# Two feed-forward layers in split fp32: block copies one tile later, weight rests first in odd tiles, statistics begun before the last products

## The chip, the cores and the metric

The kernel is one program on one core of a Trainium2 chip. The engines are TensorE (PE in the profile, PEld its weight loads), VectorE (DVE), ScalarE (ACT), GpSimd (POOL) and SyncE (SP, which issues most of the transfers). The metric is the device time of one execution in microseconds; less is better. Of the runs shown here the median counts.

## The reference, cut to what matters

A model of three layers on 512 tokens of width 1024, all in float32. Layer 0 has stick-breaking attention, layer 1 sparse attention on shared keys and values, and the last layer, which adds 16 meta tokens, has differential and grouped attention and a mixture of 16 experts. The change touches the two dense feed-forward layers, which end layers 0 and 1, and what follows each of them:

```python
def sqrelu_mlp(x, w1, w2):
    h = jax.nn.relu(x @ w1)
    return (h * h) @ w2
...
    h = h + sqrelu_mlp(rms_norm(h, norm_gain[layer, 1]), mlp_w1[layer], mlp_w2[layer])
...
return rms_norm(h, final_norm)
```

`w1` is 1024 x 4096 and `w2` 4096 x 1024. After layer 0 comes the norm of the shared keys and values. After layer 1 come two norms in a row: the first model's final norm, and then the norm `g_mix_2` that begins the last layer, whose input also holds 16 rows of meta tokens.

## The kernel before, in words

**Split numbers.** A float32 matrix product is made of three products of numbers rounded to fp32r. Each operand x is held as an upper part (a rounded copy) and a rest (x less the upper part). `mm3` (L2863) issues upper by upper, upper by rest, rest by upper. So for every operand ScalarE writes the upper part first, and VectorE then subtracts it to get the rest; TensorE needs both.

**A feed-forward layer** (m = 0 or 1) is cut in four parts (f = 0 to 3) of 1024 hidden columns. A part has two halves:
- *hidden tiles* j = 0 to 7 (`hidden` in `ff_pe`): 24 matmuls each. ScalarE makes the relu (L3099), VectorE multiplies for the square `hid_sq` (L3258).
- *products* q = 0 to 6 (`product` in `ff_pe`): the second matrix product is done by a Strassen-like scheme on 2 x 2 blocks, with seven products of 24 matmuls each. It needs sums and differences of hidden blocks (`sums`, L3242 to L3253, four short VectorE operations for each pair of tiles) and of weight blocks (`turn`, L3267, VectorE, two for each c = 0 to 3).

For a pair i of hidden tiles (2i and 2i + 1) four *block copies* n = 0 to 3 are needed. ScalarE's is `piece_upper` (L3082 to L3089), VectorE's is `piece_lower` (L3236 to L3240). Copy 0 is from the square of the even tile, copy 1 from that of the odd tile, copies 2 and 3 are those of the block sums, made after `sums`. Product 0 needs copy 0, product 1 needs copy 3, later products need the others.

**Weights.** Part f uses 22 weight buffers in a row, n = 0 to 21: one for each hidden tile, then two for each product (product q takes n = 8 + 2q and 9 + 2q). Each is loaded by SyncE to a ring of eight slots (or made by `turn`), gets its upper part from ScalarE (`ff_upper`, L2964) and its rest from VectorE (`ff_lower`, L2982), in one of four split buffers. So buffer n can be written when TensorE is through with n - 4: weight 8 in hidden tile 4, weight 12 after product 0. `ff_upper_freed` waits for that. TensorE waits for the rest with `split_w`.

**Order on VectorE** (`ff_dve`). Every engine has one fixed order of instructions. In hidden tile j: square, copy 0 or 1 of the pair, rest of weight j + 4, and in odd tiles the sums and copies 2 and 3. `turn(f, 0, n)` comes after tiles 4 and 6, `turn(f, 1, n)` for both n after tile 7. Then for each product q: `taken` (L3284) adds the two finished output banks to `h`, and then come the rests of weights 12 + 2q and 13 + 2q (of the next part where n passes 21). ScalarE's order mirrors it (`ff_act`). GpSimd only counts ring slots free (`ff_pool`), the last time when the rest of weight 21 is made.

**The end of a layer.** In layer 0 all seven products of the last part are taken in `ff_dve`, and then norm 2 follows (`flow_act`, `flow_pool`, `norm_dve`): squares of the two 512-wide halves of each 128-token tile on ScalarE, three short GpSimd operations for the reciprocal root, the scaled copy `xn` on ScalarE, eight transposes on TensorE. In layer 1 the last two products (`leave` = 2) are taken by `residual` in `flow2_dve`, mixed with the scaling of the first norm (`plain`, L660); `flow2_act` loads its table of functions, squares the meta tokens' tile, squares the first halves of all four tiles, scales the meta tile, and then works tile by tile through both norms. The `g_mix_2` norm goes in the order meta tile, 0, 1, 2, 3, and each tile's columns are split in two pieces (`x_hi` L778 on ScalarE, `x_lo` L785 on VectorE), ten pieces in all. TensorE begins the first projection of the differential attention (`df_parts`, L1568) when all splits are there; it does 24 matmuls for columns 0 to 263 and then 24 for columns 264 to 527. SyncE loads constants for the last layer after TensorE's last feed-forward matmul, and then further weights.

## Time and profile before

| | |
|---|---|
| median of 3 runs | 2543.26 us (2541.18 to 2544.34) |
| profiled execution | 2541.81 us, of which the span from first to last instruction is 2539.8 us |
| mean granted TensorE clock | 0.978 of full speed |
| busy: PE, DVE, ACT, POOL | 2377.6, 1606.2, 1100.4, 754.0 us |
| feed-forward layer 0 | from 318 to 656 us of the span |
| feed-forward layer 1 | from about 1060 to 1398 us |
| DMA | 268.46 MB, mean 106 GB/s |

Times below are microseconds from the start of the span. In a row of the timeline stand start, duration, engine, line, operation, what is written and what is read, shape and count; in brackets is how long the engine sat idle before it, and what released it. Successive matmuls overlap: each is shown at its full duration, and the next one starts before it ends.

### The profile page before, as it was taken

The numbers are of one execution on the slowest core, as the hardware profiler recorded it, in microseconds if no ns is written. First come the engines' busy times: TensorE is split into PE (matmuls) and PEld (weight loads), VectorE is DVE, ScalarE is ACT, GpSimd is POOL, SyncE is SP. The second block draws the span as 40 slices with busy tenths as digits, with TensorE's granted clock in tenths as the row PEclk, the third lists the DMA queues.
The fourth block names the chain that finished last, engine by engine and source line by source line (L and its number), as shares of the span: only waits on it lengthen the run. The fifth ranks groups of instructions, "written<-read, shape, count | busy, mean of one in ns | idle before, by whom it ended". The sixth has DMA issues, their size and how long they took to land.

```text
span 2539.8 us, 36841 instructions
## 1 busy us (share of the span) xinstructions
PE 2377.6 (94%) x13845; PEld 1890.6 (74%) x13845; DVE 1606.2 (63%) x2449; ACT 1100.4 (43%) x1986; POOL 754.0 (30%) x851
## 2 busy tenths in 40 slices
PE   7999899999999898999999799989999899899998
PEld 6777788777577665777877688879989797555555
DVE  3333277787564786487777666762067643588888
ACT  4444344444321575344445333341145401267776
POOL 7654400000007003400000644435742276411112
PEclk9999999999999899999999899999999999899999
DMA  4111223332323000332331211112210022389998
GB/s 136 53 56 50 80 79 117 116 89 78 104 88 99 18 1 7 111 83 83 116 116 43 71 51 43 46 55 67 83 42 26 26 92 87 134 290 366 362 364 300
DMA packets 267748, 268.46 MB, mean 106 GB/s; under 512 B 13258, under 2 KB 198437, under 8 KB 267603
## 3 DMA queue, kind: packets, MB, share of 16 engines
q1 hardware_dynamic: 263075, 254.04, 31.2%
q0 software_dynamic: 4528, 12.44, 1.9%
q8 instruction: 96, 1.57, 0.3%
q14 instruction: 49, 0.40, 0.1%
HBM read 256.24 MB, written 10.21 MB: 105 GB/s over the span
## 4 chain that ended last, share of the span: by engine, by line
PE 67%; DVE 16%; ACT 6%; DMA 5%; issue 5%; POOL 2%; SPq 0%; DVEq 0%; POOLq 0%; ACTq 0%
PE psum L2865 12%; PE psum L2868 12%; PE psum L2869 12%; DMA ex_tile<-in_w_down 5%; PE psum L1539 2%; PE psum L2503 2%; PE psum L2569 2%; ACT w_hi L2964 2%; PE psum L872 2%; PE psum L1254 2%; PE psum L874 2%; DVE w_lo L2982 2%; PE psum L873 2%; PE psum L1317 1%; PE psum L1309 1%
## 5 line engine op out<-in xcount | busy, mean ns | idle before, releaser
L2865 PE MATMUL psum<-x_hi,w_hi 128*128 128x264 f32 (+2 forms) x1560 | 527.2, 338 | 20.9 <-DVE x_lo L785 7.2
L2868 PE MATMUL psum<-x_lo,w_hi 128*128 128x264 f32 (+2 forms) x1560 | 517.9, 332 | 0.0
L824 POOL TENSOR_TENSOR w_hi<-ring_tile,one 128x256 fp32r<-128x256 f32 (+1 forms) x284 | 235.9, 858 | 461.0 <-PE psum L2869 429.5
L2869 PE MATMUL psum<-x_hi,ring_tile_lo 128*128 128x264 f32 (+2 forms) x1096 | 340.7, 311 | 0.0
L2865 PEld LDWEIGHTS psum<-x_hi,w_hi 128*128 128x128 f32 x1560 | 296.1, 190 | 55.9 <-issue 21.1
L2868 PEld LDWEIGHTS psum<-x_lo,w_hi 128*128 128x128 f32 x1560 | 296.3, 190 | 27.6 <-issue 1.2
L828 POOL TENSOR_TENSOR ring_tile_lo<-ring_tile,w_hi 128x256 fp32r<-128x256 f32 (+1 forms) x284 | 294.8, 1065 | 8.1
L2869 PEld LDWEIGHTS psum<-x_hi,ring_tile_lo 128*128 128x128 f32 x1096 | 208.1, 190 | 11.2
L2869 PE MATMUL psum<-x_hi,w_lo 128*128 128x512 f32 (+1 forms) x528 | 202.4, 383 | 0.0
L2865 PE MATMUL psum<-w_hi,hid_hi 128*128 128x512 f32 x448 | 176.4, 394 | 13.0 <-DVE w_lo L2982 13.0
L2964 ACT ACTIVATE w_hi<-ring_tile 128x1024 fp32r<-128x1024 f32 x128 | 130.8, 1050 | 123.2 <-PE psum L2869 112.5
L2868 PE MATMUL psum<-w_lo,hid_hi 128*128 128x512 f32 x448 | 176.7, 394 | 0.0
L2869 PE MATMUL psum<-w_hi,hid_lo 128*128 128x512 f32 x448 | 175.7, 392 | 0.0
L2982 DVE TENSOR_TENSOR w_lo<-ring_tile,w_hi 128x1024 fp32r<-128x1024 f32 x124 | 148.3, 1221 | 26.9 <-ACT w_hi L2964 26.9
L2353 DVE TENSOR_TENSOR ex_tile_lo<-ex_tile,ex_w_hi 128x1024 fp32r<-128x1024 f32 x128 | 149.5, 1218 | 15.1 <-ACT ex_w_hi L2346 13.6
L2346 ACT ACTIVATE ex_w_hi<-ex_tile 128x1024 fp32r<-128x1024 f32 x128 | 129.7, 1056 | 26.7 <-DMA ex_tile<-in_w_gate 12.4
L3088 ACT ACTIVATE hid_hi<-hid_sq 128x512 fp32r<-128x512 f32 (+1 forms) x128 | 70.5, 575 | 140.4 <-DVE hid_sq L3251 81.4
L2328 PE MATMUL psum<-ex_tile_lo,xs_hi 128*66 128x512 f32 x256 | 103.2, 403 | 15.1 <-DVE ex_tile_lo L2353 9.3
L2869 PEld LDWEIGHTS psum<-x_hi,w_lo 128*128 128x128 f32 x528 | 99.6, 189 | 19.4
L2865 PEld LDWEIGHTS psum<-w_hi,hid_hi 128*128 128x128 f32 x448 | 84.1, 188 | 35.9 <-issue 16.3
L734 POOL TENSOR_TENSOR rstd<-ssq 128x1 f32<-128x1 f32 x12 | 2.3, 191 | 357.7 <-ACT junk_ff L693 351.8
L3239 DVE TENSOR_TENSOR hid_lo<-hid_sq,hid_hi 128x512 fp32r<-128x512 f32 (+1 forms) x128 | 77.2, 624 | 45.5 <-ACT hid_hi L3088 45.5
(454 smaller groups left out, 5529.5 us busy)
## 6 DMA issues: line engine op xcount, KB each, us to landing
ring_tile<-in_mlp_w SPq DMA_DIRECT2D x128, 512.0 KB, 4.1
ex_tile<-in_w_gate SPq DMA_DIRECT2D x64, 512.0 KB, 12.4
ex_tile<-in_w_up SPq DMA_DIRECT2D x64, 512.0 KB, 12.0
ex_tile<-in_w_down SPq DMA_DIRECT2D x64, 512.0 KB, 12.0
ring_tile<-in_w_in SPq DMA_DIRECT2D x52, 512.0 KB, 3.8
ring_tile<-in_sb_w_qkv SPq DMA_DIRECT2D x24, 512.0 KB, 3.8
ring_tile<-in_nsa_w_kv SPq DMA_DIRECT2D x12, 512.0 KB, 3.8
ring_tile<-in_sb_w_o SPq DMA_DIRECT2D x8, 512.0 KB, 3.3
```

What stands on the lines that cost most here:

```text
L824: last = pool.tensor_tensor(hi[:, cols], raw[:, cols], one[:, :].broadcast_to([P, D // len(parts)]), ALU.mult)
L828: last = pool.tensor_tensor(lo[:, cols], raw[:, cols], hi[:, cols].bitcast(F32), ALU.subtract)
L2328: first = pe.matmul(dst, xs_hi[:, u, k, :], lo[:, k % 2, :], start=(k == 0), stop=False)
L2346: act.activation(ex_w_hi[:, n, :], ex_ring.wait(act, name, j + n, turn), ACT.Copy).then_inc(ex_wh, 1)
L2353: dve.tensor_tensor(ex_tile_lo[:, slot, :], ex_tile[:, slot, :], ex_w_hi[:, n, :].bitcast(F32), ALU.subtract).then_inc(ex_ws, 1)
L2865: upper = pe.matmul(dst, a_hi, b_hi, start=first, stop=False, skip_group_check=True)
L2868: pe.matmul(dst, a_hi, b_lo, start=False, stop=False, skip_group_check=True)
L2869: return pe.matmul(dst, a_lo, b_hi, start=False, stop=final, skip_group_check=True)
L2964: act.activation(hi, raw, ACT.Copy).then_inc(split_w_hi, 1)
L2982: eng.tensor_tensor(lo, raw, hi.bitcast(F32), ALU.subtract).then_inc(split_w, 1)
L3088: act.activation(hid_piece(hid_hi[i], first, last), sq_piece(i, half, rows).rearrange("p (a n) -> p a n", n=SEQ // 2), ACT.Copy).then_inc( ...
L3239: dve.tensor_tensor(hid_piece(hid_lo[i], first, last), sq_piece(i, half, rows).rearrange("p (a n) -> p a n", n=SEQ // 2), hid_piece(hid_hi ...
```

## The change

In the hidden tiles of both layers, copies 2 and 3 of a pair, upper parts and rests alike, move from the odd tile that makes the sums to the even tile after it (for the last pair, to behind the eight tiles). In odd tiles the upper part and the rest of weight j + 4 come ahead of copy 1. `turn(f, 0, 1)` moves from tile 6 to tile 4, `turn(f, 1, 0)` from behind tile 7 to tile 6; `turn(f, 1, 1)` stays behind the tiles.

In the last part, `taken` of product 5 is cut in two: its first half (tile 0) comes between the rests of weights 20 and 21, for both layers. In layer 0 the rest follows as before; in layer 1 it is left to `flow2_dve`, which no longer has `residual(0)`.

ScalarE gets a piece of the next norm ahead of the upper parts of weights 20 and 21 of the last part: the table load and the first half-squares of tiles 0 and 1, and in layer 1 also the meta tile's square.

TensorE's first projection of the differential attention waits only for 8 of the 10 splits (meta tile and tiles 0 to 2) before its first 24 matmuls, and for all 10 before the next 24.

```diff
--- before.py
+++ after.py
@@ -597,7 +597,7 @@
         def place(u, t):
             return PLACE[t] if u == 6 else t
 
-        def flow2_act(act):
+        def flow2_act(act, first=False):
 
             def square(u, t, c):
                 r = rows_of(t)
@@ -620,12 +620,18 @@
                     act.wait_ge(norm_tp, 2 * (norm_base(6) + n - 1))
                 act.activation(xn[0:r, n % 2, :], h[0:r, t, :], ACT.Copy, scale=rstd[0:r, t:t + 1]).then_inc(norm_xn, 1)
 
-            act.preload_act_table_set(LN_EXP)
-            whole(6, QT)
-            act.wait_ge(norm_sq, squared(6, QT))
-            for t in range(QT):
-                act_t.inc(square(5, t, 0))
-                act.wait_ge(act_step, act_t.value())
+            def halves(tiles):
+                for t in tiles:
+                    act_t.inc(square(5, t, 0))
+                    act.wait_ge(act_step, act_t.value())
+
+            if first:
+                act.preload_act_table_set(LN_EXP)
+                whole(6, QT)
+                act.wait_ge(norm_sq, squared(6, QT))
+                halves(range(2))
+                return
+            halves(range(2, QT))
             scaled(QT)
             for s in range(8):
                 if s < QT:
@@ -663,7 +669,6 @@
                 residual_tile(dve, H_ALL - UPD, 1, t, half_banks)
 
             dve.wait_ge(gain_in, 16)
-            residual(0)
             residual(1)
             plain(0)
             residual(2)
@@ -679,12 +684,8 @@
 
         HALVED = (1, 2, 4, 5, 7)
 
-        def flow_act(act, u, updated=None):
-
-            base, halves = norm_base(u), u in HALVED
-            act.preload_act_table_set(LN_EXP)
-
-            def square(t, c):
+        def flow_square(act, u, updated, t, c):
+                halves = u in HALVED
                 cols = slice(c * D // 2, (c + 1) * D // 2) if halves else slice(0, D)
                 if u == 0:
                     act.wait_ge(tile_in[t], 16)
@@ -693,10 +694,22 @@
                 return act.activation((junk if u in (0, 1) else junk_ff)[:, cols], h[:, t, cols], ACT.Square, scale=D ** -0.5,
                                       accum_out=ssq[:, c, t:t + 1])
 
+        def first_squares(act, u, updated, tiles):
+            for t in tiles:
+                act_t.inc(flow_square(act, u, updated, t, 0))
+                act.wait_ge(act_step, act_t.value())
+
+        def flow_act(act, u, updated=None, begun=0):
+
+            base, halves = norm_base(u), u in HALVED
+            if not begun:
+                act.preload_act_table_set(LN_EXP)
+
+            def square(t, c):
+                return flow_square(act, u, updated, t, c)
+
             if halves:
-                for t in range(QT):
-                    act_t.inc(square(t, 0))
-                    act.wait_ge(act_step, act_t.value())
+                first_squares(act, u, updated, range(begun, QT))
             if u in FF_NORMS:
                 for j in range(2):
                     if u == 1:
@@ -1570,6 +1583,8 @@
             for n in range(3):
                 w = split2_wait(pe, "df", 4 * hd + n, 0, SPLIT_BASE["df"] + hd * 3 + n, w2_hi[:, (hd + n) % 2, :])
                 for c in range(2):
+                    if hd == n == 0 and c:
+                        pe.wait_ge(split_x, split_base(7))
                     if n == 0 and c == 0:
                         pe.wait_ge(v2_l, hd + 1)
                     elif hd == 0:
@@ -3028,7 +3043,7 @@
             pe.wait_ge(norm_ev, 2 * (norm_base(6) + T2))
             pe.wait_ge(ff_freed, 2)
             ring.wait(pe, "df", 6)
-            pe.wait_ge(split_x, split_base(7))
+            pe.wait_ge(split_x, split_base(6) + 2 * QT)
             for _ in df_parts(pe, 0):
                 pass
             pe.wait_ge(b2_ready, 1)
@@ -3078,7 +3093,7 @@
         HID_PIECES = (("A11", "A11", 0, slice(0, SEQ // 2)), ("A12", "A22", 1, slice(0, SEQ)),
                       ("S2", "S3", 0, slice(0, SEQ)), ("S4", "S1", 1, slice(0, SEQ)))
 
-        def ff_act(act, m, upd):
+        def ff_act(act, m, upd, early):
             def piece_upper(f, i, n):
                 first, last, half, rows = HID_PIECES[n]
                 if n < 2:
@@ -3097,12 +3112,19 @@
                     act.wait_ge(ff_mm, n + 1)
                     act.wait_ge(ff_hid, n + 3)
                     act.activation(relu[:, j % 2, :], ff_hid_bank(f, j)[:, :], ACT.Relu).then_inc(ff_relu, 1)
+                    if j % 2 == 0 and j:
+                        piece_upper(f, j // 2 - 1, 2)
+                        piece_upper(f, j // 2 - 1, 3)
+                    if j % 2:
+                        ff_upper_freed(act, m, upd, f, j + SPLITS)
                     piece_upper(f, j // 2, j % 2)
-                    ff_upper_freed(act, m, upd, f, j + SPLITS)
-                    if j % 2:
-                        piece_upper(f, j // 2, 2)
-                        piece_upper(f, j // 2, 3)
+                    if j % 2 == 0:
+                        ff_upper_freed(act, m, upd, f, j + SPLITS)
+                piece_upper(f, FF_PAIRS - 1, 2)
+                piece_upper(f, FF_PAIRS - 1, 3)
                 for q in range(len(PRODUCTS)):
+                    if f == FF_PARTS - 1 and q == 4:
+                        early()
                     for n in (FF_TILES + SPLITS + 2 * q, FF_TILES + SPLITS + 2 * q + 1):
                         if n < FF_STREAM:
                             ff_upper_freed(act, m, upd, f, n)
@@ -3122,15 +3144,19 @@
             for p in range(PAIRS):
                 sb_act(act, p)
             flow_act(act, 1, H_BEFORE[1] - QT)
-            ff_act(act, 0, UPD)
-            flow_act(act, 2, H_BEFORE[2] - QT)
+            def second_norm():
+                act.preload_act_table_set(LN_EXP)
+                first_squares(act, 2, H_BEFORE[2] - QT, range(2))
+
+            ff_act(act, 0, UPD, second_norm)
+            flow_act(act, 2, H_BEFORE[2] - QT, 2)
             kv_act(act)
             gates_act(act)
             act.preload_act_table_set(LN_EXP)
             queries_act(act)
             nsa_act(act)
             flow_act(act, 4, H_BEFORE[4] - QT)
-            ff_act(act, 1, H_BEFORE[4])
+            ff_act(act, 1, H_BEFORE[4], lambda: flow2_act(act, True))
             flow2_act(act)
             act.wait_ge(b2_in, B2_CONST)
             act.wait_ge(lam_d, 1)
@@ -3257,12 +3283,15 @@
                 dve.wait_ge(ff_relu, n + 5)
                 dve.scalar_tensor_tensor(hid_sq[:, i % 2, j % 2, :], ff_hid_bank(f, j)[:, :], 0.0, relu[:, j % 2, :],
                                          ALU.max, ALU.mult).then_inc(ff_hid, 1)
-                piece_lower(f, i, j % 2)
+                if j % 2 == 0 and j:
+                    piece_lower(f, i - 1, 2)
+                    piece_lower(f, i - 1, 3)
+                if j % 2 == 0:
+                    piece_lower(f, i, 0)
                 lower(f, j + SPLITS)
                 if j % 2:
+                    piece_lower(f, i, 1)
                     sums(f, i)
-                    piece_lower(f, i, 2)
-                    piece_lower(f, i, 3)
 
             def turn(f, c, n):
                 first = ff_raw(dve, m, f, (B12, B22, B22, B21)[c] + n)
@@ -3270,7 +3299,7 @@
                 dst = ff_difference(m, f, n) if c == 2 else w2_turn[:, n, :]
                 dve.tensor_tensor(dst, first, other, ALU.subtract).then_inc(ff_t, 1)
 
-            def taken(f, q):
+            def taken(f, q, which=(0, 1)):
                 n, rows = ((1, (0, 1)), (0, (2, 3)), (0, (0, 1)), (0, (0, 1)), (0, (2, 3)), (1, (0, 1)), (1, (2, 3)))[q]
                 name = PRODUCTS[q][1]
                 if q < 3:
@@ -3278,6 +3307,8 @@
                 elif q == 3:
                     dve.wait_ge(ff_ev, EV_0 + ff_part(m, f, 3) + 3)
                 for c, t in enumerate(rows):
+                    if c not in which:
+                        continue
                     if q >= 3:
                         dve.wait_ge(acc_done, upd + f * UPD + n * QT + t + 1)
                     hs = h[:, t, 512 * n:512 * n + 512]
@@ -3292,17 +3323,27 @@
             for f in range(FF_PARTS):
                 for j in range(FF_TILES):
                     hidden(f, j)
-                    if j in (4, 6):
-                        turn(f, 0, (j - 4) // 2)
-                for n in range(2):
-                    turn(f, 1, n)
-                for q in range(len(PRODUCTS) - (leave if f == FF_PARTS - 1 else 0)):
+                    if j == 4:
+                        turn(f, 0, 0)
+                        turn(f, 0, 1)
+                    if j == 6:
+                        turn(f, 1, 0)
+                last = f == FF_PARTS - 1
+                piece_lower(f, FF_PAIRS - 1, 2)
+                piece_lower(f, FF_PAIRS - 1, 3)
+                turn(f, 1, 1)
+                for q in range(len(PRODUCTS) - (2 if last else 0)):
                     taken(f, q)
                     for n in range(2):
+                        if last and q == 4 and n:
+                            taken(f, 5, (0,))
                         lower(f, FF_TILES + SPLITS + 2 * q + n)
                     if q in (1, 3):
                         for n in range(2):
                             turn(f, 2 if q == 1 else 3, n)
+            if not leave:
+                taken(FF_PARTS - 1, 5, (1,))
+                taken(FF_PARTS - 1, 6)
 
         @block.vector
         def _(dve):
```

## Rows read from the trace of the kernel before

**Rows 1.** Waits of PE, whole span: total, times, longest in us.
```profile
PE psum L2865 <- DVE w_lo L2982: 13.0, 8, 1.6
...
PE psum L2865 <- DVE x_lo L785: 7.2, 3, 6.6
```

**Rows 2.** Busy time by stretch, from one such wait's end to the next.
```profile
375.49:459.71 84.22, 82.59 (x360) 67.52 (x361) 65.07 (x85) 35.00 (x47) 0.00 (x0) 1.00 0.34 100
```

**Rows 3.** Timeline of PE around product 2 of the first part.
```profile
373.46 0.40 PE L2869 MATMUL psum<-w_hi,hid_lo 128*128 128x512 f32 x1
375.49 0.48 PE L2865 MATMUL psum<-w_hi,hid_hi 128*128 128x512 f32 x1 [1.63 <-DVE w_lo L2982]
375.80 0.40 PE L2868 MATMUL psum<-w_lo,hid_hi 128*128 128x512 f32 x1
```

**Rows 4.** Timeline of DVE, first part, tile 7 to product 2.
```profile
363.94 0.68 DVE L3258 SCALAR_TENSOR_TENSOR hid_sq<-psum,relu 128x512 f32<-128x512 f32 x1
...
367.41 0.42 DVE L3247 TENSOR_TENSOR hid_sq<-hid_sq 128x256 f32<-128x256 f32 x1
...
369.45 1.29 DVE L3239 TENSOR_TENSOR hid_lo<-hid_sq,hid_hi 128x512 fp32r<-128x512 f32 x2 [0.24 <-ACT hid_hi L3088]
370.66 2.35 DVE L3271 TENSOR_TENSOR w_turn<-ring_tile,w_turn 128x1024 f32<-128x1024 f32 x2
372.93 1.28 DVE L3284 TENSOR_TENSOR h<-psum,h 128x512 f32<-128x512 f32 x2
374.13 2.35 DVE L2982 TENSOR_TENSOR w_lo<-w_turn,w_hi 128x1024 fp32r<-128x1024 f32 x2
```

**Rows 5.** Timeline of ACT, the relu of tile 7 in the first part.
```profile
362.83 0.60 ACT L3099 ACTIVATE relu<-psum 128x512 f32<-128x512 f32 x1 [1.20 <-PE psum L2869]
```

**Rows 6.** Timeline of ACT, POOL and DVE at the end of layer 1's feed-forward.
```profile
1381.18 2.01 ACT L2964 ACTIVATE w_hi<-ring_tile 128x1024 fp32r<-128x1024 f32 x2 [3.51 <-PE psum L2869]
...
1386.73 2.01 ACT L2964 ACTIVATE w_hi<-w_turn 128x1024 fp32r<-128x1024 f32 x2 [3.53 <-PE psum L2869]
...
1388.02 2.35 DVE L2982 TENSOR_TENSOR w_lo<-w_turn,w_hi 128x1024 fp32r<-128x1024 f32 x2
...
1388.75 1.28 ACT L623 ACT_TABLE_LOAD   x1
...
1391.23 0.63 ACT L609 ACTIVATE junk_ff<-h 128x512 f32<-128x512 f32 x1
1391.28 0.22 POOL L651 TENSOR_SCALAR rstd<-ssq 128x1 f32<-128x1 f32 x1 [335.01 <-ACT junk_ff L609]
...
1391.59 0.57 POOL L653 TENSOR_TENSOR rstd<-rstd,neg_half 128x1 f32<-128x1 f32 x1
...
1392.29 0.69 DVE L3221 TENSOR_TENSOR h<-psum,h 128x512 f32<-128x512 f32 x1 [1.32 <-PE psum L2869]
...
1394.25 1.15 ACT L621 ACTIVATE xn<-h,rstd 16x1024 f32<-16x1024 f32 x1
...
1395.31 0.61 ACT L609 ACTIVATE junk_ff<-h 128x512 f32<-128x512 f32 x1
```

**Rows 7.** Timeline of all engines, first transposes of tile 0 after layer 1.
```profile
1402.94 1.97 PE L796 MATMUL psum<-ident,xn 128*128 128x128 f32 x8 [4.52 <-ACT xn L621]
```

**Rows 8.** The chain that ended last, up to the first projection.
```profile
1417.58 2.12 DVE x_lo L785 x2
```

**Rows 9.** Timeline of PE, the first projection's first matmuls.
```profile
1420.06 0.56 PE L2865 MATMUL psum<-x_hi,w_hi 128*128 128x264 f32 x1 [6.61 <-DVE x_lo L785]
...
1423.44 0.28 PE L2865 MATMUL psum<-x_hi,w_hi 128*128 128x264 f32 x1
1423.56 0.28 PE L2868 MATMUL psum<-x_lo,w_hi 128*128 128x264 f32 x1
```

**Rows 10.** Busy time by stretch ahead of it: engines, then PEclk, DMA share, GB/s.
```profile
1415.00:1418.00 3.00, 0.00 (x0) 0.00 (x0) 3.00 (x5) 1.23 (x2) 3.00 (x4) 0.76 0.00 0
```

**Rows 11.** Timeline of DVE at the end of layer 0's feed-forward.
```profile
656.21 0.69 DVE L3284 TENSOR_TENSOR h<-psum,h 128x512 f32<-128x512 f32 x1 [2.10 <-PE psum L2869]
```

## The prediction

> **What bounds the kernel now.** I read the page's busy shares first: TensorE is at work for 94% of the span, so only what shortens TensorE's idle time, or the work around it, can move the end. Then the waits of TensorE over the whole span [rows 1]. The reader is to see one reason that returns: eight waits for a weight's rest (L2982), 13.0 us together, none over 1.63. A view of TensorE's gaps puts one in each feed-forward part, always ahead of product 2. The stretches from one to the next are 84.22 us long with 82.59 of work [rows 2]; that is one of six, 84.21 to 84.24. The other wait of size is a single one of 6.61 us for `x_lo`, ahead of the attention of the last layer [rows 9]; before it stands one of 4.52 us for the scaled tile 0 [rows 7].
>
> **Why product 2 waits.** In the first part ScalarE's relu of tile 7 ends at 363.43 [rows 5]. VectorE starts the square only at 363.94, because `turn` was in its way, and then works without a real pause: sums from 367.41, copies 2 and 3 from 369.45, two turns from 370.66, take of product 0 from 372.93, rest of weight 12 from 374.13 [rows 4]. TensorE's last matmul of product 1 starts at 373.46 and the next at 375.49 [rows 3].
>
> **What one such stall is worth.** The profile's 1.63 us counts from the end of a matmul that the next one would have overlapped. Matmuls start 0.23 us apart, though each shows 0.40: 84.22 less the stall is some 82.4 for 360 of them, 0.229 [rows 2]. Without the wait the next would start at 373.69, so 1.80 is lost; the first behind it holds up its successor by 0.31 in place of 0.23 [rows 3], another 0.08. I take 1.88 for each part. From below it is the 1.63 of the idle column.
>
> **Part 1: the new order in hidden tiles.** Nothing is added: each part has the same copies, sums, turns and rests. What goes is VectorE's waiting for ScalarE between its own steps. Start-to-start times from [rows 4]: a turn or a rest 1.14 (370.66 to 372.93 is two), the take of two banks 1.20, two copies 1.21 (369.45 to 370.66), a square 0.61 (half of that pair, same size), four sums with the wait to copy 2 2.04 (367.41 to 369.45). New sequence behind tile 7, with one `turn` gone from tile 6: square at 363.46 (relu's end and 0.03). ScalarE copies weight 11 at once, 363.34 to 364.38, 1.04 as in [rows 6] (2.01 for two, which overlap a little); rest 11 at 364.42; copy 1 at 365.56, its end 0.69 later at 366.25; sums at 366.28 and so copies 2 and 3 at 368.32; `turn(f, 1, 1)` at 369.53; take of product 0 at 370.66; rest 12 at 371.86, done at 373.08. The release of TensorE took 0.14 in the old order (374.13 + 1.22 to 375.49), so weight 12 is there at 373.22, and 373.69 is when TensorE can want it. The stall goes, with 0.47 us in hand. Is VectorE behind before tile 7? In tile 4 it now has square 0.61, copies 2 and 3 1.21, copy 0 0.4, rest 1.14 with some 0.3 of waiting, two turns 2.27: 5.9 for a tile of 24 x 0.229 = 5.5; tile 5 has square, rest, copy 1 and sums, 0.61 + 1.14 + 0.65 + 1.8 (the 2.04 less its 0.24 of waiting) = 4.2, and makes up the 0.4. Tile 6 has one turn, 4.8. So tile 7 starts on time. Ring loads are no obstacle: weight 12's slot is freed by the rest of weight 4, six tiles ahead of the turn that now reads it.
>
> **What is late next.** Product 1 needs copy 3 of the last pair for its last quarter, a quarter of 24 matmuls before 373.69, at 372.3; its rest ends at 369.61. Behind product 2 every VectorE step is 2.3 us earlier than before and TensorE 1.9, so no later product gets tighter; they had no wait. Gain of this part 8 x 1.88 = 15.0 us; bounds 13.0 (idle column), and if the 0.47 in hand were not there but 0.5 lacking, 8 x 1.4 = 11.
>
> **Part 2: cover in the last part.** Product 5's first half ends one half product before its second, which VectorE sees at 1392.29: 12 x 0.23 earlier is 1389.51. The early statistics run on ScalarE from 1383.20 (behind the pair of 1381.18) and take, from the old places, table and meta square 2.48 (1388.75 to 1391.23) and two half-squares of 0.755 (four were 3.02, 1391.23 to 1394.25): until 1387.20, against 1386.73 for the old start of weights 20 and 21 [rows 6]. Rest 20 then starts at 1388.28 (0.26 late), the take of tile 0 at 1389.51, rest 21 at 1390.11, ready at 1391.47. Product 6 can start at 1392.09. So the layer's last product doesn't wait, with 0.6 in hand; in layer 0 there is no meta square, and more in hand.
>
> The Trainium skill ("ScalarE: Activation LUTs", What ACT_TABLE_LOAD costs) gives a table load some 1.38 us of draining behind its 1.28, for a switch of sets. Here the next instruction follows at 1.30, meta square and all inside the 2.48. By the page the early work would end 1.38 later and product 6 wait some 0.6 us at the end of layer 1; by the rows it doesn't.
>
> **Part 3: what the early work earns.** In layer 0 the transposes of tiles 0 and 1 wait for nothing but TensorE's own last product; the chain then goes from that product through VectorE's take at 656.21 [rows 11], the gains, ScalarE's raw copies, and only then the third tile's square. None of it starts earlier. Gain 0. In layer 1 TensorE's products end at 1397.8 (1392.29 and 24 x 0.23), but the chain lies on ScalarE: weights 20 and 21, table, meta square, four half-squares, meta scaling at 1394.25, tile 0's second half at 1395.31 [rows 6]. New: weights done at 1389.2, two half-squares until 1390.7. Then the meta scaling needs GpSimd's root, and GpSimd is held in its counting loop until rest 21 is done, 1391.33; its two operations took 0.88 (1391.28 to 1392.16), so 1392.25 at best; scaling 1.06; tile 0's half-square at 1393.4. That is 1.9 earlier; I take 1.8 for GpSimd's release. Everything behind goes in the same order and shifts along (TensorE's final banks are there at 1395.1 and 1397.9, before they are taken). Bounds: 0, were a hidden wait next, and 3.5, were GpSimd not in the way.
>
> **Part 4: the projection.** TensorE now waits for eight splits, not ten. The last two take 2.12 us [rows 8], so it starts at 1417.94, or 1416.14 with part 3, in place of 1420.06. Columns 0 to 263 lie in tiles 0 to 2, and the next 24 matmuls come over 2.9 us later, when the last splits (1418.0 by then) are done. The DMAs, tied to the last product and so not shifted, are over before 1415 [rows 10]. Gain 2.1, from 1.9 (half of four pieces) to 2.12. The granted clock was at its lower level, 1.2 GHz, for the first 15 matmuls, 0.225 apart, then 2.4 with 0.12 [rows 9], after the idle stretch before it [rows 10]. That costs 15 x 0.105 = 1.6 now; with a shorter idle stretch (4.6 in place of 6.6) it can be from 0 to 2.5 (all 24). I take the same.
>
> The Trainium skill ("TensorE: Matmul & The Clock Gate", HAM oscillation) lets an idle stretch drop the clock; if the shorter one no longer did, 1.6 more would be won.
>
> **Sum.** 15.0 + 1.8 + 2.1 = 18.9 us off the profiled execution's 2541.81 (its span and 2.0 around it), 2522.9. The median of the runs lies 1.45 above that execution; from 2543.26 the same sum gives 2524.4. After this the kernel's later stages follow TensorE and each other, so they move as a whole.
>
> **The rivals.**
> - *The stalls stay in part.* 0.47 us in hand is one short VectorE operation. For it: all eight parts have it alike, so 0.1 missing costs 0.8. Against it: the durations hardly vary. With 0.5 to 1.5 left per part, 2528 to 2536; 2530 as its centre. Chance 0.13.
> - *The ends earn nothing.* Rest 21 or GpSimd's root comes later than reckoned, product 6 waits, and the chain to `x_lo` doesn't move: parts 3 and 4 give 0 to 2, time 2526.5 to 2528.5. The page's drain is of this kind, 2525. For it: GpSimd's 335 us of waiting ends at [rows 6] only by the meta square, so its release by rest 21 was never seen. Chance 0.08.
> - *The clock pays.* No drop in part 4, and other drops fall elsewhere: 2520 to 2523. The spread of three runs before is 3.2. Chance 0.07.
> - *Slower: copy 3 of the last pair comes too late for product 1.* The place is behind tile 7, where copies 2 and 3 now stand in both queues. I have 2.7 us in hand. Were the copies 6.6 late (a tile, 5.5, and a turn), product 1 would stall 3.9 in each part, 31 us: 2555.6. It outweighs the 18.9 from a stall of 2.4 on, so from 5.1 us of lateness. Against it: everything ahead of these copies is ready earlier than now. Chance 0.02.
> - *The change doesn't do what it says*: product 2's stall is as long, because another step of VectorE's fills the time. Only the ends move: 2539. Chance 0.03.
>
> **How the numbers follow.** My forecast, all of parts 1 to 4, has 0.67; time 2524.4, own range 2522.5 to 2527. The range goes down to the clock's rival and up into the partial stalls: 2520.5 to 2532. About what a measurement can tell from no change is 0.2%, 5 us: 2538.2 to 2548.3. Inside it lie most of "doesn't do what it says" and a tail of the first rival, 0.04; above it 0.02; below 0.94.
>
> **What the new profile would show.** No wait for L2982 in TensorE's list; stretches from one product 2 to the next of 82.3 us; `hid_sq` of tile 7 0.03 behind its relu; VectorE idle 2 us more in products. At layer 1's end: the table load before weights 20 and 21, tile 0's second half-square some 1.9 us nearer to the last product, the wait ahead of the first transposes 2.7 in place of 4.52, the wait ahead of the projection 4.5 in place of 6.6. Wrong would be: a new wait of L2865 for `hid_lo`, a wait of product 6 for rest 21, or an unchanged end with the stalls gone, which would mean a later stage has its own clock.

## The result and the profile after

The changed kernel takes 2524.28 us, the median of 5 runs (2522.70 to 2525.09). The kernel before, run beside it, takes 2542.01 us (5 runs, 2535.99 to 2544.34). The ratio is 0.9932, with a 95% interval of 0.9917 to 0.9946: faster, by 17.7 us. The profiled execution of the changed kernel took 2525.02 us with a span of 2523.2, against 2541.81 and 2539.8 before.

TensorE's waits over the whole span, the lines that answer to [rows 1, 7, 9]:

```profile
PE psum L809 <- ACT xn L621: 6.1, 3, 2.9
...
PE psum L2880 <- DVE x_lo L798: 5.1, 3, 4.5
```

The eight waits for a weight's rest, 13.0 us of idle time, are gone from the list, and the single wait ahead of the last layer's projection has shrunk from 6.6 to 4.5. The stretch from the first part's product 2 to the second's, which answers to [rows 2], is now all work, and 1.87 shorter:

```profile
373.26:455.61 82.35, 82.35 (x362) 67.62 (x360) 64.89 (x85) 34.27 (x46) 0.00 (x0) 1.00 0.35 103
```

All six such stretches measure 82.35. VectorE's timeline behind tile 7, which answers to [rows 4]:

```profile
363.02 0.69 DVE L3284 SCALAR_TENSOR_TENSOR hid_sq<-psum,relu 128x512 f32<-128x512 f32 x1 [0.79 <-ACT relu L3114]
...
363.97 1.23 DVE L2997 TENSOR_TENSOR w_lo<-w_turn,w_hi 128x1024 fp32r<-128x1024 f32 x1 [0.26 <-ACT w_hi L2979]
...
367.88 1.29 DVE L3265 TENSOR_TENSOR hid_lo<-hid_sq,hid_hi 128x512 fp32r<-128x512 f32 x2 [0.24 <-ACT hid_hi L3103]
369.09 1.22 DVE L3300 TENSOR_TENSOR w_turn<-ring_tile,w_turn 128x1024 f32<-128x1024 f32 x1
370.23 1.28 DVE L3315 TENSOR_TENSOR h<-psum,h 128x512 f32<-128x512 f32 x2
371.43 2.35 DVE L2997 TENSOR_TENSOR w_lo<-w_turn,w_hi 128x1024 fp32r<-128x1024 f32 x2
```

The square now follows its relu, and has idled 0.79 for it: VectorE is in time. Rest 12 starts 8.41 behind the square, where it was 10.19 before. It is done 1.22 into the last row, at 372.65, which with the release of 0.14 makes weight 12 ready at 372.79. TensorE takes it up when its own order allows:

```profile
373.03 0.39 PE L2884 MATMUL psum<-w_hi,hid_lo 128*128 128x512 f32 x1
373.26 0.39 PE L2880 MATMUL psum<-w_hi,hid_hi 128*128 128x512 f32 x1
```

These answer to [rows 3]: 0.23 from one start to the next, no idle time, and 0.47 us between 372.79 and 373.26.

At the end of layer 1, the timeline of ScalarE, VectorE and GpSimd that answers to [rows 6]:

```profile
1368.87 1.28 ACT L629 ACT_TABLE_LOAD   x1
1370.17 1.06 ACT L609 ACTIVATE junk_ff<-h 16x1024 f32<-16x1024 f32 x1
...
1372.86 2.01 ACT L2979 ACTIVATE w_hi<-w_turn 128x1024 fp32r<-128x1024 f32 x2
...
1375.18 0.69 DVE L3315 TENSOR_TENSOR h<-psum,h 128x512 f32<-128x512 f32 x1
1375.79 1.22 DVE L2997 TENSOR_TENSOR w_lo<-w_turn,w_hi 128x1024 fp32r<-128x1024 f32 x1
...
1377.28 0.22 POOL L657 TENSOR_SCALAR rstd<-ssq 128x1 f32<-128x1 f32 x1 [327.27 <-DVE w_lo L2997]
...
1378.24 1.15 ACT L621 ACTIVATE xn<-h,rstd 16x1024 f32<-16x1024 f32 x1 [2.01 <-POOL rstd L659]
1379.30 0.61 ACT L609 ACTIVATE junk_ff<-h 128x512 f32<-128x512 f32 x1
```

The table load stands ahead of weights 20 and 21, which start at 1372.86. GpSimd, held before by the meta square [rows 6], is now released by VectorE's rest 21, and ScalarE idles 2.01 us for GpSimd's root before it scales the meta tile. TensorE's rows behind it, which answer to [rows 7, 9]:

```profile
1386.94 1.09 PE L809 MATMUL psum<-ident,xn 128*128 128x128 f32 x8 [2.85 <-ACT xn L621]
...
1402.01 0.56 PE L2880 MATMUL psum<-x_hi,w_hi 128*128 128x264 f32 x1 [4.49 <-DVE x_lo L798]
...
1404.79 0.42 PE L2880 MATMUL psum<-x_hi,w_hi 128*128 128x264 f32 x1
...
1405.33 0.28 PE L2880 MATMUL psum<-x_hi,w_hi 128*128 128x264 f32 x1
```

The idle times are 2.85 for 4.52, and 4.49 for 6.61. The projection still begins at the lower clock (1.2 GHz): matmuls start some 0.22 apart until 1405.01, then 0.12, 14 of them slow where there were 15. The granted clock was 0.50 of full speed from 1402 to 1405.

### The profile page after: what moved, and what is told of

Same layout as the page of the kernel before. It is cut to its first block, busy times and chain, and to the rows that moved or that the text cites. A ratio compares the mean times of both kernels' runs of the same rounds, so it can differ in the third digit from the quotient of the medians.

```text
span 2523.2 us, 36839 instructions
## 1 busy us (share of the span) xinstructions
PE 2374.5 (94%) x13845; PEld 1890.0 (75%) x13845; DVE 1605.6 (64%) x2449; ACT 1093.6 (43%) x1986; POOL 745.8 (30%) x851
## 4 chain that ended last, share of the span: by engine, by line
PE 77%; DVE 10%; DMA 6%; ACT 3%; issue 3%; POOL 2%; SPq 0%; DVEq 0%; POOLq 0%; ACTq 0%
PE psum L2880 16%; PE psum L2883 16%; PE psum L2884 16%; DMA ex_tile<-in_w_down 5%; PE psum L1552 2%; PE psum L2518 2%; PE psum L2584 2%; PE psum L885 2%; PE psum L1267 2%; PE psum L887 2%; PE psum L886 2%; PE psum L1330 1%; PE psum L1322 1%; PE psum L2527 1%; PE psum L2343 1%
## 5 line engine op out<-in xcount | busy, mean ns | idle before, releaser
L2880 PE MATMUL psum<-x_hi,w_hi 128*128 128x264 f32 (+2 forms) x1560 | 527.2, 338 | 18.9 <-DVE k_lo L1816 7.1
L3114 ACT ACTIVATE relu<-psum 128x512 f32<-128x512 f32 x64 | 38.3, 598 | 189.8 <-PE psum L2884 189.8
L2348 PE MATMUL psum<-ex_w_hi,xs_lo 128*66 128x512 f32 x256 | 101.8, 398 | 0.0
L2349 PE MATMUL psum<-ex_w_hi,xs_hi 128*66 128x512 f32 x256 | 101.5, 396 | 0.0
```

Of the source, the lines that this page charges most:

```text
L2348: pe.matmul(dst, xs_lo[:, u, k, :], hi[:, k % 2, :], start=False, stop=False)
L2349: last = pe.matmul(dst, xs_hi[:, u, k, :], hi[:, k % 2, :], start=False, stop=(k == KT - 1))
L2880: upper = pe.matmul(dst, a_hi, b_hi, start=first, stop=False, skip_group_check=True)
```

## The experiments

Three lengths are read from TensorE's timeline in each kernel: a *part* (product 2 to the next part's product 2, all six), the *end* (first matmul of the last product 2 to tile 0's first transposes, layer 1), and the *projection* (from those transposes to the first matmul of the projection). The end starts just behind the last stall. So in a kernel with stalls it also holds the 0.08 by which a stall delays the second matmul [rows 3]. That is why 33.16 stands beside 33.07, and 31.45 to 31.49 beside 31.38, with nothing else different.

| kernel | part | end | projection | median, lowest to highest | ratio to before (95%) |
|---|---|---|---|---|---|
| before | 84.22 | 33.16 | 17.11 | 2542.01, above | |
| changed | 82.35 | 31.38 | 15.08 | 2524.28, above | 0.9932 (0.9917 to 0.9946) |
| order only | 82.35 | 33.07 | 17.13 | 2526.34, 2522.39 to 2527.87 | 0.9948 (0.9931 to 0.9966) |
| ends only | 84.23 | 31.45 | 15.08 | 2535.08, 2530.92 to 2538.65 | 0.9985 (0.9975 to 0.9995) |
| turns back | 83.08 | 31.48 | 15.10 | 2529.47, 2528.86 to 2530.61 | 0.9962 (0.9950 to 0.9975) |
| turns only | 84.23 | 33.16 | 17.10 | 2539.89, one run | |
| nothing early in layer 0 | 82.35 | 31.38 | 15.07 | 2522.63, 2522.08 to 2523.91 | 0.9939 (0.9922 to 0.9955) |
| odd tiles back | 82.62 | 31.49 | 15.09 | 2523.84, 2522.05 to 2525.88 | 0.9922 (0.9905 to 0.9938) |
| short operation added | 82.35 | 31.37 | 15.07 | 2521.55, one run | |
| long operation added | 83.09 | 31.48 | 15.09 | 2530.01, 2529.60 to 2531.31 | 0.9948 (0.9931 to 0.9964) |
| root early | 82.35 | 29.70 | 15.29 | 2521.61, 2519.68 to 2524.06 | 0.9913 (0.9896 to 0.9929) |
| root early, no load wait | 82.35 | 29.70 | 14.94 | 2522.88, 2521.52 to 2524.30 | 0.9920 (0.9906 to 0.9933) |
| changed again | 82.35 | 31.40 | 15.10 | 2522.08, 2518.04 to 2523.09 | 0.9910 (0.9895 to 0.9925) |

The kernel before, run in three groups, gave 2539.27 (2535.24 to 2543.97) beside order only, ends only, turns back and nothing early in layer 0; 2543.19 (2537.7 to 2544.6) beside odd tiles back, the two added operations and root early; and 2542.68 (2535.95 to 2546.65) beside the other three. The lengths above hold within 0.04 in every part; the medians of the kernel before move by 4 us.

### The order alone

The kernel before with the new order of copies, rests and turns in the hidden tiles, and nothing at the layers' ends.

```diff
 # kernel before: hidden() and ff_act() with the changed order
+                if j % 2 == 0 and j:
+                    piece_lower(f, i - 1, 2)
+                    piece_lower(f, i - 1, 3)
...
+                    if j == 4:
+                        turn(f, 0, 0)
+                        turn(f, 0, 1)
+                    if j == 6:
+                        turn(f, 1, 0)
```

> The kernel before with the new order in the hidden tiles alone (copies, weight rests, turns); layer ends and the projection's wait as before. My account: the wait of TensorE for the rest of weight 12 is gone in all eight parts, 1.88 us each, so 15.0 us less than before (about 2528 where before is 2543); the stretch from one product 2 to the next is 82.3 us; the wait ahead of the first transposes of tile 0 after layer 1 stays 4.5 and that ahead of the projection 6.6. Rival (the parts aren't independent, the order needs the shorter ends): less than 13 us. Rival (part of the gain comes from elsewhere): more than 16 us.

The parts are 82.35 long as in the changed kernel, the end and the projection as in the kernel before. TensorE's waits in this kernel:

```profile
PE psum L2865 <- DVE x_lo L785: 7.5, 3, 6.9
...
PE psum L796 <- ACT xn L621: 6.9, 3, 4.5
```

The two waits of the ends stay, 6.9 and 4.5, and no wait for a weight's rest is left. The order alone takes away all the stalls of the parts.

The median fell by 12.9 and not by 15.0, which by the number alone is the rival's case (less than 13). The trace speaks against the rival's reason, since the stalls are gone without the shorter ends. Where the other 2 us may be is told in the last section: in stretches behind the feed-forward layers that were longer here.

### The ends alone

The changed kernel with the old order in the hidden tiles: early squares, the cover in the last part, and eight splits ahead of the projection remain.

```diff
 # changed kernel: hidden() and ff_act() back to the old order
-                if j % 2 == 0 and j:
-                    piece_lower(f, i - 1, 2)
-                    piece_lower(f, i - 1, 3)
...
+                    if j in (4, 6):
+                        turn(f, 0, (j - 4) // 2)
```

> The changed kernel with the old order in the hidden tiles: early statistics, product 5 taken in two halves, and the projection's shorter wait stay. My account: eight waits for the rest of weight 12, 1.6 us each in the idle column, stretches of 84.2 us; from the layer end 1.8 us and from the projection 2.0, 3.8 us less than before in all, which is below what a timing can tell (0.2%) but plain in the trace. Rival (the ends earn nothing by themselves): the two waits stay 4.5 and 6.6 us.

```profile
PE psum L2880 <- DVE w_lo L2997: 13.1, 8, 1.6
```

That line of TensorE's waits is [rows 1] again, while end and projection are 1.7 and 2.0 shorter. Each set of edits keeps its own saving without the other: 1.87 in each part for the order, 3.7 at the end of layer 1 for the ends (1.71 and 2.03). By the medians they are worth 12.9 and 4.2 against the kernel before run beside them, 17.1 together where both at once gave 17.7.

### The turns at their old places

```diff
 # changed kernel
-                    if j == 4:
-                        turn(f, 0, 0)
-                        turn(f, 0, 1)
-                    if j == 6:
-                        turn(f, 1, 0)
+                    if j in (4, 6):
+                        turn(f, 0, (j - 4) // 2)
...
-                turn(f, 1, 1)
+                for n in range(2):
+                    turn(f, 1, n)
```

> The changed kernel, with the turns at their old places: turn(f, 0, 1) after tile 6 and both turn(f, 1, n) behind the last copies. My account by the same sum: two turns behind the copies put the rest of weight 12 at 374.36 on the first part's old scale, where TensorE wants it at 373.69, so a stall of 0.67 and 0.08 behind it returns in each part: 6.0 us more than the changed kernel. Rival (the copies' move alone removed the stall, the turns are off the path): no difference, under 1 us. Rival (the turns' move alone did it): the full 15 us come back.

```profile
373.79:456.89 83.10, 82.61 (x360) 67.52 (x361) 64.98 (x85) 34.29 (x47) 0.00 (x0) 1.00 0.34 102
```

This is the stretch by engine of the first part. A second turn behind tile 7 costs 1.14 on VectorE, 0.47 was in hand, and this part is 0.75 longer (0.71 to 0.75 over the six). TensorE's idle column grows by 0.49 only (83.10 less 82.61).

### The turns alone

The kernel before with the turns at their new places and the old order of copies and rests.

```diff
 # kernel before
-                    if j in (4, 6):
-                        turn(f, 0, (j - 4) // 2)
-                for n in range(2):
-                    turn(f, 1, n)
+                    if j == 4:
+                        turn(f, 0, 0)
+                        turn(f, 0, 1)
+                    if j == 6:
+                        turn(f, 1, 0)
+                turn(f, 1, 1)
```

> The kernel before with only the turns at their new places (both turn(f, 0, n) after tile 4, turn(f, 1, 0) after tile 6), copies and weight order as before. My account: VectorE has no slack in tiles 4 to 7 in the old order, 4.4 us of steps and waits for an even tile with one turn and 6.7 for an odd one, 11.1 for 11.0 of TensorE's, so a turn moved ahead only pushes the rest back: the step from one product 2 to the next stays 84.2 us, and the square of tile 7 comes 1.1 later. Rival (moving the turn away from product 2 is what helps): 83.1 us a part.

The stall before product 2 stands unchanged, at the end of tile 7's chain:

```profile
374.72 0.47 PE L2865 MATMUL psum<-w_hi,hid_hi 128*128 128x512 f32 x1 [1.63 <-DVE w_lo L2982]
```

```profile
362.06 0.60 ACT L3099 ACTIVATE relu<-psum 128x512 f32<-128x512 f32 x1
```

```profile
363.17 1.22 DVE L3271 TENSOR_TENSOR w_turn<-ring_tile,w_turn 128x1024 f32<-128x1024 f32 x1
364.31 0.68 DVE L3258 SCALAR_TENSOR_TENSOR hid_sq<-psum,relu 128x512 f32<-128x512 f32 x1
```

On VectorE the turn now placed in tile 6 starts at 363.17, because tile 6 runs late. The relu of tile 7 ends at 362.66, and the square starts at 364.31, 1.65 behind it, where it was 0.51 in the kernel before (363.94 behind 363.43 [rows 4, 5]). One turn fewer behind tile 7 is paid for by one turn that still stands in tile 7's way. By itself the move of the turns is worth nothing; with the new order of copies and rests it is worth 0.75 a part.

### The odd tiles as before

The changed kernel, but in odd tiles the block's first copy again ahead of the weight's rest, on both engines.

```diff
 # changed kernel, ff_act (hidden() in the same way)
-                    if j % 2:
-                        ff_upper_freed(act, m, upd, f, j + SPLITS)
                     piece_upper(f, j // 2, j % 2)
-                    if j % 2 == 0:
-                        ff_upper_freed(act, m, upd, f, j + SPLITS)
+                    ff_upper_freed(act, m, upd, f, j + SPLITS)
```

> The changed kernel, except that in odd tiles copy 1 comes before the upper part and the rest of weight j + 4 again, as it was; the copies one tile later and the turns' new places stay. My account: VectorE waits again for ScalarE inside tile 7, 0.66 us in all, so the rest of weight 12 is ready at 373.88 on the first part's old scale against the 373.69 that TensorE can use: each part some 0.2 to 0.27 us longer than in the changed kernel, 2 us in all, though the idle column shows next to nothing. Rival (the order in odd tiles carries a third of the gain or more): 5 us or more. Rival (it is idle decoration): 0.

```profile
373.47:456.10 82.63, 82.61 (x360) 67.53 (x361) 64.81 (x85) 34.63 (x46) 0.00 (x0) 1.00 0.34 102
```

The part is 0.27 longer, with 0.02 of idle time shown. So this edit is worth 0.27 of the 1.88 a part, 2.2 us over the eight, too little to be told in the medians here.

### How much is in hand: a short and a long operation

A VectorE addition into a buffer that nothing reads any more, ahead of the turn behind tile 7. It adds work to the computation and changes no output.

```diff
 # changed kernel; the long one with relu[:, :, :]
+                dve.tensor_tensor(relu[:, 1, 0:256], relu[:, 1, 0:256], relu[:, 1, 0:256], ALU.add)
                 turn(f, 1, 1)
```

> The changed kernel with one extra VectorE addition of 256 numbers a partition (0.35 us from start to start) behind the last copies of every part; it writes where nothing is read any more. My account: 0.47 us are in hand at that place, so the step from one product 2 to the next stays 82.34 us and the time is the changed kernel's. Rival (VectorE is the pace setter there and nothing is in hand): 0.35 us more in each part, 2.8 in all.

```profile
371.90:454.27 82.37, 82.37 (x362) 67.60 (x362) 65.22 (x86) 34.24 (x46) 0.00 (x0) 1.00 0.34 103
```

```profile
367.72 0.42 DVE L3334 TENSOR_TENSOR relu<-relu 128x256 f32<-128x256 f32 x1
368.06 1.22 DVE L3300 TENSOR_TENSOR w_turn<-ring_tile,w_turn 128x1024 f32<-128x1024 f32 x1
```

The short operation pushes the turn by 0.34 (367.72 to 368.06), which is less than the 0.47 in hand, and it costs nothing: the part stays at 82.35 within 0.02.

> The same with an extra addition of 1024 numbers a partition (1.14 us from start to start). My account: 1.14 less the 0.47 in hand leaves 0.67, and 0.08 behind it: each part 0.75 us longer than in the changed kernel, 6.0 in all, the same as with the turns at their old places. Rival (more is in hand, the sums with waits between the engines were too careful): under 0.4 a part. Rival (nothing is in hand): 1.1 to 1.2 a part.

```profile
374.25:457.33 83.08, 82.59 (x360) 67.54 (x361) 66.03 (x86) 34.30 (x47) 0.00 (x0) 1.00 0.34 102
```

```profile
PE psum L2880 <- DVE w_lo L2997: 3.9, 8, 0.5
```

```profile
369.43 1.22 DVE L3334 TENSOR_TENSOR relu<-relu 128x1024 f32<-128x1024 f32 x1
370.56 1.22 DVE L3300 TENSOR_TENSOR w_turn<-ring_tile,w_turn 128x1024 f32<-128x1024 f32 x1
```

These are the first part's stretch, TensorE's waits and VectorE's timeline in the kernel with the long one. It pushes the turn by 1.13 and brings the eight waits back, 0.5 each in TensorE's list. The part is 0.74 longer: 1.13 less the 0.47 in hand, and the 0.08 of the next matmul [rows 3].

### Nothing early in layer 0

```diff
 # changed kernel
-            ff_act(act, 0, UPD, second_norm)
-            flow_act(act, 2, H_BEFORE[2] - QT, 2)
+            ff_act(act, 0, UPD, lambda: None)
+            flow_act(act, 2, H_BEFORE[2] - QT)
```

> The changed kernel without the early table load and half-squares in layer 0 (they go back to the place behind weights 20 and 21); layer 1 keeps them. My account: layer 0's end hangs on TensorE's last product, not on ScalarE, so nothing changes: the first transposes of the third tile start equally long after the last product, and the time is that of the changed kernel within 0.5 us. Rival (the early squares help both layers alike): 1.5 to 2 us more.

TensorE's row behind layer 0, the transposes of the third tile, first in this kernel and then in the changed one:

```profile
651.43 1.09 PE L809 MATMUL psum<-ident,xn 128*128 128x128 f32 x8 [2.51 <-ACT xn L730]
```

```profile
652.49 1.09 PE L809 MATMUL psum<-ident,xn 128*128 128x128 f32 x8 [2.51 <-ACT xn L730]
```

The same 2.51 of idle time: the early squares of layer 0 earn nothing.

### GpSimd's root ahead of its last counts

In layer 1's last part, GpSimd takes the meta tile's root before it counts the splits of weights 20 and 21.

```diff
 # changed kernel, ff_pool (flow2_pool then does the other tiles)
                 for j in range(2 * FF_TILES):
+                    if m == 1 and f == FF_PARTS - 1 and j == 2 * FF_TILES - 2:
+                        flow2_root(pool, 6, QT)
                     pool.wait_ge(split_w, ff_no(m, f, read[j]) + 1)
```

> The changed kernel with GpSimd's two operations for the meta tile's root ahead of its last two counts of layer 1, in place of behind them. My account: in the changed kernel the meta tile's scaling waits until the rest of weight 21 frees GpSimd; here it follows ScalarE's half-squares of tiles 2 and 3, so tile 0's second half-square starts 1.6 us earlier and the wait ahead of the first transposes falls from 2.85 to some 1.3: 1.6 us less, up to 1.8. Rival (tile 1's last bank or GpSimd's later roots are next at once): under 0.5 us less.

Timelines of this kernel: GpSimd's root, ScalarE's meta scaling, and TensorE's two rows that it leads to:

```profile
1371.87 1.25 POOL L655 TENSOR_SCALAR rstd<-ssq 128x1 f32<-128x1 f32 x1 [321.39 <-ACT junk_ff L609]
...
1376.74 1.15 ACT L621 ACTIVATE xn<-h,rstd 16x1024 f32<-16x1024 f32 x1
```

```profile
1385.72 1.09 PE L811 MATMUL psum<-ident,xn 128*128 128x128 f32 x8 [1.17 <-ACT xn L621]
...
1401.01 0.56 PE L2882 MATMUL psum<-x_hi,w_hi 128*128 128x264 f32 x1 [5.04 <-DMA ring_tile<-in_w_in]
```

The meta scaling has no idle time before it any more, and the end is 1.68 shorter. GpSimd's wait for rest 21 was what stopped the gain of the end at 1.7. But the projection now waits for a load, and 0.21 of it is given back there.

### The same without the wait for the load

```diff
 # kernel of the experiment above, projection of the last layer on TensorE
-            ring.wait(pe, "df", 6)
```

The load of projection weight 6 is already waited for by those who split it.

> The kernel with GpSimd's root early, and without TensorE's wait for the seventh load ahead of the projection (GpSimd waits for each load before it splits it, so TensorE needs none). My account: the 0.2 us that the load took back of the 1.7 come too: 29.7 us from the last product 2 to the first transposes, 15.1 to the projection, 1.7 us less than the changed kernel in the trace; as a time that is inside what a measurement can tell, between 0 and 3 us less. Rival (something else that the load's wait hid comes next, such as the split of the first weight on GpSimd): the projection's start stays 15.3 behind the transposes.

```profile
1399.67 0.56 PE L2882 MATMUL psum<-x_hi,w_hi 128*128 128x264 f32 x1 [4.72 <-DVE x_lo L800]
```

The projection is 14.94, released by the splits again. Why it is 0.16 below the one of the changed kernel run beside it isn't known. Both stretches together are 1.86 shorter than in the changed kernel run beside it (44.64 for 46.50). As a time that isn't seen: 2522.88 against 2522.08, with overlapping runs.

### The changed kernel again

The changed kernel itself, run beside the one above.

> The changed kernel itself, timed beside the kernel before and beside the next one on the same chip: 17 to 19 us less than before; stretches of 82.35 us; 31.4 us from the last product 2 to the first transposes of tile 0, 15.1 from there to the projection.

Its three lengths repeat within 0.02, its median is 2522.08, and the ratio 0.9910. It is 20.6 us below the kernel before, outside the 17 to 19 that were expected. So a median of this kernel moves by some 2 us between groups of runs, and the ranking of the last four kernels of the table by their times says nothing.

## Why the prediction was right

The time forecast was 2524.4 and 2524.28 was measured, in the own range of the likeliest case (2522.5 to 2527). Step by step:

- **What a stall is worth.** Forecast 1.88 a part from matmul starts, against 1.63 of the idle column. Measured: the parts shrank by 1.87, and the start of TensorE's product 2 moved forward by 1.87 to 1.90 at a time. Other kernels show the same gap: 0.49 idle and 0.74 to 0.75 lost (long operation, turns back), 0.02 idle and 0.27 lost (odd tiles back). The idle column leaves out the overlap of back-to-back matmuls, 0.17, and 0.08 of the matmul after, about 0.25 in each case, for stalls of 0.02 to 1.63 idle. Eight stalls of 1.88 give the 15.0 of the forecast.
- **The new order on VectorE.** Square to rest 12 was reckoned at 8.40 and is 8.41. The slack of 0.47 is 0.47 in the row, and three kernels bracket it: an operation that fits inside costs nothing, and one turn more (1.14) or the long operation (1.13) costs 0.75 and 0.74, which is what goes beyond the slack, and the 0.08 of the matmul after. Of the 1.88, the turns' places are worth 0.75 and the odd tiles' order 0.27, each with the other edits in place; the parts aren't additive, for the turns alone are worth nothing.
- **Tile 7 starts on time.** VectorE idles 0.79 before the square. The turns-only kernel shows what was avoided: with the old order of copies, tile 6's turn holds the square up.
- **The cover in the last part.** Product 6 does not wait. Weights 20 and 21 start 3.99 behind the table load on ScalarE, forecast 4.00. Rest 21 is done at 1377.01 and ready at 1377.15; product 6 starts at 1377.76, so 0.61 is in hand, forecast 0.6. No run takes product 5 in one piece or leaves out only layer 1's early squares, so what each of them does by itself is read from the rows and not shown apart. The meta square follows the start of the load by 1.30, and product 6 has no wait. The drain that the Trainium skill gives for a switch of sets ("ScalarE: Activation LUTs", What ACT_TABLE_LOAD costs) was the wrong price for this place: the load before this one, at 996.81, names the same set, so nothing is switched. Where the changed kernel does switch, ahead of a sigmoid in the last layer, the trace doesn't agree with the page either, for the next operation starts 1.30 behind the load's start:

```profile
1713.78 1.28 ACT L1867 ACT_TABLE_LOAD   x1
1715.08 0.61 ACT L1867 ACTIVATE sig<-psum 128x528 f32<-128x528 f32 x1
```

- **Layer 0's early work.** Forecast 0. The wait for the third tile is 2.51 with it and without it.
- **Layer 1's end.** Forecast 1.8, measured 1.7: the table's 1.78 holds the 0.08 of the last stall, which the 15.0 count already, and against order only the end is 1.69 shorter. GpSimd's wait for rest 21 was the bound, as reckoned: rest 21 ended at 1377.01 (1375.79 and 1.22) and GpSimd began at 1377.28, 0.27 later. The forecast had 1.9 with next to nothing for this release and took off 0.1; the 0.27 is what it had too small. With the root early the end is 1.68 shorter still, 3.4 in all, where the bound without GpSimd in the way was 3.5.
- **The projection.** Forecast 2.1, measured 2.04 against the chain at the transposes. Its lower clock cost 14 slow matmuls in place of 15.
- **The sum against the profile.** 18.9 was forecast for the profiled execution, which fell by 16.8 (2541.81 to 2525.02). The savings of the steps are there: 15.0, 1.7 and 2.0, which is 18.7. Feed-forward layer 0 also began 0.9 earlier in this execution, where nothing is changed yet, and layer 1's first hidden tiles took 0.3 less. Against that, three stretches with the same work were longer: the hidden tiles of layer 0's first part by 0.5 (45.1 for 44.6), the stretch from the transposes behind layer 0 to layer 1's feed-forward by 1.5 (404.8 for 403.3), and the one from the projection's first matmul to the end by 1.4 (1121.2 for 1119.8). The first of these arises in the first 25 matmuls, where no edit acts yet, and the last is 1119.8 in the changed kernel run again. The middle one is 404.4 there, and the last section says why the change isn't cleared of it. So the later stages did not move quite "as a whole", as the forecast had them. The medians fell by 17.7, and by 20.6 with the changed kernel run again (2542.68 to 2522.08); 18.9 lies between. That the median came within 0.1 of the forecast is chance: nothing here is known to better than 2 us.

The rivals: the stalls did not stay in part (no idle time in any of the six stretches). The ends did earn, in the changed kernel and alone. The clock paid nothing to speak of at the projection (14 slow matmuls for 15), with an idle stretch of 4.49 for 6.61 ahead of it. Copy 3 of the last pair is no wait of TensorE's: its rest ends at 369.17 (367.88 and 1.29), and TensorE's waits have no line for `hid_lo`. The change does what it says.

## What to carry to other kernels

A stall of TensorE cost the idle time shown plus some 0.25 us here, because back-to-back matmuls overlap, so judge it by the starts of the matmuls at two marks and not by the idle column. Before moving a step, write its engine's queue as a chain of start-to-start times with the slack at its end: here the whole win, its 0.47 in hand, and the price of one turn too many came out of a few rows. And look for the engine in a counting loop: a wait that a queue makes for a later stage (GpSimd's for rest 21) can hold up what is ready. Last, compare the stretches behind a change too, in every kernel at hand: here the saving upstream came with a longer stretch downstream (last section).

## What the runs showed of the hardware

**Stretches at the lower clock fall differently from one execution to the next.** The first 3 us of layer 0's feed-forward, by engine, with the granted clock as the third number from the end, in the kernel before and then in the changed one:

```profile
318.03:321.03 3.00, 3.00 (x24) 2.90 (x24) 3.00 (x6) 2.51 (x4) 0.00 (x0) 1.00 0.56 211
```

```profile
317.10:320.10 3.00, 3.00 (x17) 3.00 (x16) 3.00 (x6) 2.51 (x4) 0.00 (x0) 0.56 0.53 195
```

The same matmuls run at full clock in one execution, at 0.56 of it in the other, and 17 rather than 24 fit. No edit acts yet at this place. Over the kernels of the table, the time from the first of these matmuls to the 25th is 3.51 to 4.11 us. After the projection the order-only kernel and the changed one show the same kind of difference:

```profile
1404.00:1414.00 10.00, 9.99 (x59) 10.00 (x60) 4.46 (x13) 0.20 (x1) 3.97 (x7) 0.69 0.00 1
```

```profile
1402.00:1412.00 10.00, 9.99 (x70) 10.00 (x71) 6.52 (x19) 0.20 (x1) 7.30 (x11) 0.84 0.12 35
```

In the first 10 us, 59 matmuls run at a mean clock of 0.69, and 70 at 0.84. From the projection's first matmul to the 354th it is 49.8 to 50.0 us in eleven kernels, 52.1 in order only and 51.6 in turns only. These two have the long idle time ahead of the projection (6.9 and 6.5), but so has the kernel before (6.6), at 49.8. So a long idle time doesn't always cost these 2 us; whether it makes them likelier, one execution of each kernel can't show. What decides where a drop falls was not found. A difference of 1 to 4 us of this kind hides the 1.86 that were won in the trace (root early, no load wait).

**A stretch that is longer in every kernel with the new order.** From the transposes behind layer 0 to layer 1's first feed-forward matmul TensorE has the same matmuls in every kernel. It takes 403.3 us in the kernel before, 401.3 in ends only and 400.8 in turns only. In the ten others, which all move the copies to the next tile, it takes 404.0 to 404.8. A part of the difference stands at one place, where TensorE waits for VectorE's `blocks` (in the kernel before and then in the changed one):

```profile
763.52 2.69 PE L985 MATMUL psum<-blocks,ring_tile 128*128 128x124 f32 x22 [1.72 <-DVE blocks L1026]
```

```profile
756.00 2.32 PE L998 MATMUL psum<-blocks,ring_tile 128*128 128x124 f32 x12 [2.13 <-DVE blocks L1039]
```

The wait is 2.13 to 2.15 in the ten, and 1.72, 0.45 and 0.45 in the three. VectorE's sixteen operations for it take 5.60 to 5.62 us in the ten, and 5.19, 3.92 and 3.92 in the three, while GpSimd works beside it in all of them. So 0.7 to 4 us of what the order wins may be given back here, which would fit the 12.9 of order only. Why it should be isn't known, and with so few traces (one of each kernel, two of the changed one) it is not shown that the order is the cause.

**GpSimd beside VectorE.** GpSimd's operation on 128x1 takes 0.22 us at 1377.28, when VectorE is idle, and 1.25 in the kernel with the early root, at 1371.87. VectorE's row there:

```profile
1370.69 2.35 DVE L3304 TENSOR_TENSOR w_turn<-ring_tile,w_turn 128x1024 f32<-128x1024 f32 x2
```

The two turns end at 1373.04 and GpSimd's operation at 1373.12. It ended 0.08 behind VectorE. That agrees with the Trainium skill ("SBUF — State Buffer", SBUF: two separate sides), where GpSimd and VectorE have a port in common that VectorE can hold. Nothing was lost by it, for the early root had 2.97 us until its reader at 1376.74 (from its second operation's end, 1373.77).
